# Log decays of a head: broadcast by a matmul, or copied over all partitions by DMA

## The reference, cut to what matters

```python
acs = jnp.cumsum(dtc * a.reshape(g, r), axis=2)          # log decay of every token
seg = acs_t[..., :, None] - acs_t[..., None, :]
decay_in = jnp.exp(jnp.where(lower, seg, -jnp.inf))       # 128 x 128 for one head
cb = jnp.einsum('bcign,bcjgn->bcgij', cc, bc)             # one for a group
y_diag = jnp.einsum('bcgij,bcgrij,bcjgrp->bcigrp', cb, decay_in, xdt)
```

## Time and profile before

| | |
|---|---|
| median of 3 runs | 2887.86 us (2879.88 to 2888.41) |
| the profiled execution | 2884.6 us, of which the span of the trace is 2882.7 us |
| TensorE, matmuls | 2811.8 us, 98% of the span |
| TensorE, weight loads | 2386.9 us, 83% |
| VectorE | 1769.8 us, 61% |
| ScalarE | 1483.7 us, 51% |
| GpSimd | 204.2 us, 7% |
| mean granted clock of TensorE | 0.995 |
| DMA | 594.25 MB, mean 206 GB/s |

### The profile page before, as it was taken

How to read it: one execution, slowest core, us unless ns; L and a number is a source line. 1 busy time by engine, 2 the same in 40 slices (tenths; PEclk the granted TensorE clock), 3 DMA queues, 4 the chain that set the end, 5 groups by cost and what they waited for, 6 DMA issues and landing times.

```text
span 2882.7 us, 41663 instructions
## 1 busy us (share of the span) xinstructions
PE 2811.8 (98%) x16960; PEld 2386.9 (83%) x16960; DVE 1769.8 (61%) x2255; ACT 1483.7 (51%) x2210; POOL 204.2 (7%) x259
## 2 busy tenths in 40 slices
PE   7999999999999999999899999999999999999998
PEld 4888998888777888877669889988887888897886
DVE  2487899886344445544355878998854444554555
ACT  3356776774333445533334567767743434544443
POOL 0001111120000000000100011111200000000000
PEclk9999999999999999999999999999999999999999
DMA  9945455546777644567796454555467565554665
GB/s 391 341 156 167 162 169 175 176 154 201 281 278 288 203 152 161 170 249 274 265 347 189 158 166 159 171 174 175 154 205 284 192 201 171 161 176 153 204 220 174
DMA packets 166591, 594.25 MB, mean 206 GB/s; under 512 B 20244, under 2 KB 22548, under 8 KB 166016
## 3 DMA queue, kind: packets, MB, share of 16 engines
q1 hardware_dynamic: 155376, 558.24, 56.3%
q0 software_dynamic: 10960, 33.34, 4.0%
q10 hardware_dynamic: 64, 0.02, 0.0%
HBM read 577.85 MB, written 13.66 MB: 205 GB/s over the span
## 4 chain that ended last, share of the span: by engine, by line
PE 84%; DVE 7%; DMA 5%; ACT 1%; issue 1%; SPq 0%; DVEq 0%; POOLq 0%; POOL 0%; ACTq 0%
PE PM L414 18%; PE PM L426 17%; PE PM L415 17%; PE PM L419 7%; PE PM L430 7%; PE PM L420 7%; PE A L639 5%; DVE w_l L392 2%; DVE arena L1368 2%; PE A L451 2%; DVE X L1408 2%; DMA Zt<-in_w_mod 2%; DMA raw<-in_w_in 2%; DMA raw<-in_w_out 1%; PE A L636 1%; PE PM L636 1%
## 5 line engine op out<-in xcount | busy, mean ns | idle before, releaser
L392 DVE TENSOR_TENSOR w_l<-raw,w_h 128x1024 fp32r<-128x1024 f32 (+1 forms) x880 | 1057.2, 1213 | 980.2 <-ACT w_h L387 971.4
L387 ACT ACTIVATE w_h<-raw 128x1024 fp32r<-128x1024 f32 (+1 forms) x880 | 903.6, 1046 | 837.9 <-PE PM L426 298.7
L414 PE MATMUL PM<-w_h,hT_h 128*128 128x512 f32 x1408 | 563.8, 400 | 2.2 <-issue 1.4
L415 PE MATMUL PM<-w_h,hT_l 128*128 128x512 f32 x1408 | 549.9, 391 | 0.0
L419 PE MATMUL PM<-hT_h,w_h 128*128 128x256 f32 x1920 | 486.4, 291 | 5.7 <-ACT w_h L387 2.5
L420 PE MATMUL PM<-hT_l,w_h 128*128 128x256 f32 x1920 | 469.7, 282 | 0.0
L414 PE MATMUL PM<-w_h,Z 128*128 128x512 f32 x1024 | 406.9, 397 | 12.7 <-ACT w_h L387 9.1
L415 PE MATMUL PM<-w_h,Z 128*128 128x512 f32 x1024 | 401.4, 392 | 0.0
L419 PEld LDWEIGHTS PM<-hT_h,w_h 128*128 128x128 f32 x1920 | 366.5, 191 | 20.6 <-issue 12.0
L426 PE MATMUL PM<-w_l,hT_h 128*128 128x512 f32 x1408 | 377.6, 390 | 0.7 <-DVE w_l L392 0.7
L420 PEld LDWEIGHTS PM<-hT_l,w_h 128*128 128x128 f32 x1920 | 367.2, 191 | 6.2 <-issue 4.8
(11 more groups left out here) (189 smaller groups left out, 2205.8 us busy)
## 6 DMA issues: line engine op xcount, KB each, us to landing
raw<-in_w_in SPq DMA_DIRECT2D x608, 512.0 KB, 4.0
raw<-in_w_ps SPq DMA_DIRECT2D x128, 512.0 KB, 5.0
raw<-in_w_mod SPq DMA_DIRECT2D x112, 512.0 KB, 4.1
Zt<-in_w_mod SPq DMA_DIRECT2D x80, 512.0 KB, 14.2
raw<-in_w_pa SPq DMA_DIRECT2D x64, 512.0 KB, 4.5
raw<-in_w_out SPq DMA_DIRECT2D x64, 512.0 KB, 6.0
arena<-in_states POOLq DMA_DIRECT2D x16, 512.0 KB, 3.8
out_state_f_out<-arena POOLq DMA_DIRECT2D x16, 256.0 KB, 2.8
```

The costliest lines, as they stand in the source:

```text
L387: act.activation(w_h[:, k % RING, :, 0:n], half_raw(k, n), ACT.Copy).then_inc(hi_ready, 1)
L392: dve.tensor_tensor(w_l[:, k % RING, :, 0:n], half_raw(k, n), w_h[:, k % RING, :, 0:n].bitcast(F32), ALU.subtract).then_inc(lo_ready, 1)
L414: pe.matmul(tok_out(s), hi[:, kt, tk], wh, start=kt == 0, stop=False, skip_group_check=True)
L415: pe.matmul(tok_out(s), lo[:, kt, tk], wh, start=False, stop=False, skip_group_check=True)
```

## The change

The broadcast of a head's log decays leaves TensorE. The rows are made once per layer without their second copy (4 matmuls fewer), ScalarE copies them from PSUM to `Hs` (64 partitions x 512) and stores them to a scratch tensor in HBM. For every head, GpSimd's queue then issues a DMA that reads the head's row of 2 KB and writes it to all 128 partitions of the buffer `E[h % 4]` (`decay_row`). `exp` reads and writes that buffer. Its step moves for heads 0 to 3 from 2 + h to 1 + h, so `exp(q, 0)` stands at 1, ahead of `z_silu`; heads 4 to 7 stay at 2 + h. The rows of heads 4 to 7 are issued when `y_diag` of head h - 4 is done, those of the next group's heads 0 to 3 at the end of `ssd_group`, ahead of the loading of its states. `squares` writes its unused output to `zs` in place of `E[0]`.

```diff
-                        for w in range(2):
-                            mm = fp32(A[NH * w:NH * w + NH, 0, ds * P:(ds + 1) * P], SA[:, 8 + ds, :], (Umat, Lmat)[ds // 2], ds == 0)
+                        mm = fp32(A[0:NH, 0, ds * P:(ds + 1) * P], SA[:, 8 + ds, :], (Umat, Lmat)[ds // 2], ds == 0)
...
-                def decay(q, h):
-
-                    if h == 0:
-                        pe.wait_ge(s_("H_ready"), L + 1)
-                        if q == 0:
-                            pe.wait_ge(s_("cb_even"), L * 4 + 4)
-                            pe.wait_ge(s_("cb_odd"), L * 4 + 4)
-                        else:
-                            pe.wait_ge(s_("st_stored"), L * NG + q)
-                    if h >= 2:
-                        pe.wait_ge(s_("exp_done"), (L * NG + q) * HG + h - 1)
-                    b = A[:, 2 + h % 2, :]
-                    mm = pe.matmul(b, sel[:, q * HG + h:q * HG + h + 1].to_broadcast([P, P]), H[:].rearrange("p d s n -> p (d s n)"),
-                                   start=True, stop=True, skip_group_check=True)
-                    mm.then_inc(s_("decay_done"), 1)
...
-                def H_hi():
+                def H_copy():
                     act.wait_ge(s_("acsT_done"), L + 1)
-                    act.activation(H[:].rearrange("p d s n -> p (d s n)"), A[:, 0, :], F.Copy).then_inc(s_("H_hi"), 1)
+                    act.activation(Hs[:], A[0:NH, 0, :], F.Copy).then_inc(s_("H_copied"), 1)
+                    act.wait_ge(s_("H_copied"), L + 1)
+                    act.dma_start(h_dram[L], Hs[:]).then_inc(s_("H_stored"), DMA)
...
                 def exp(q, h):
                     G = L * NG + q
-                    act.wait_ge(s_("decay_done"), G * HG + h + 1)
-                    if h >= 4:
-                        act.wait_ge(s_("y_part"), G * HG + h - 3)
+                    act.wait_ge(e_loaded[h % 4], (G * 2 + h // 4 + 1) * DMA)
                     e = E[h % 4]
                     for d in range(2):
                         for s in range(2):
-                            ins = act.activation(e[:, d, s, :], A[:, 2 + h % 2, (2 * d + s) * P:(2 * d + s + 1) * P],
-                                                 F.Relu, scale=-1.0, bias=SA[:, 2 * d + s, q * HG + h:q * HG + h + 1])
+                            ins = act.activation(e[:, d, s, :], e[:, d, s, :], F.Relu, scale=-1.0,
+                                                 bias=SA[:, 2 * d + s, q * HG + h:q * HG + h + 1])
...
                     for h in range(HG):
-                        st[2 + h] = [lambda h=h: exp(q, h)] + st.get(2 + h, [])
+                        at = 1 + h + h // 4
+                        st[at] = [lambda h=h: exp(q, h)] + st.get(at, [])
...
-                def H_lo():
-                    dve.wait_ge(s_("H_hi"), L + 1)
...
+                def decay_row(q, h):
+
+                    G = L * NG + q
+                    if q == 0 and h == 0:
+                        wait_alone(pool, s_("H_stored"), (L + 1) * DMA)
+                    if q or h >= 4:
+                        wait_alone(pool, s_("y_part"), G * HG + h - 3)
+                    row = h_dram[L, q * HG + h:q * HG + h + 1, :].to_broadcast([P, 4 * P])
+                    pool.dma_start(E[h % 4].rearrange("p d s n -> p (d s n)"), row).then_inc(e_loaded[h % 4], DMA)
+
                 def ssd_group(q):
...
                     ins.then_inc(s_("xw_ready"), 1)
+                    decay_row(q, 4)
                     if q:
                         wait_alone(pool, s_("yT_done"), G)
                     for s in range(2):
+                        if s:
+                            decay_row(q, 5)
...
                     ins.then_inc(s_("yD_ready"), 1)
+                    decay_row(q, 6)
+                    decay_row(q, 7)
                     if q < NG - 1:
+                        for h in range(4):
+                            decay_row(q + 1, h)
                         wait_alone(pool, s_("yoff_done"), G + 1)
                         load_states(q + 1)
```

More of the change, by code:

```diff
@@ L239, in build @@
         x_dram = nc.dram_tensor("x_scratch", (2, TOK, D_MODEL), F32).ap()
+        h_dram = nc.dram_tensor("log_decay_scratch", (DEPTH, NH, 4 * P), F32).ap()
         gate_dram = nc.dram_tensor("gate_scratch", (2, D_MODEL), F32).ap()
@@ L311, in build @@
         fng = part(2048, 5376)
-        sel32 = part(NH, 4864)
         modg = part(512, 0).rearrange("p (t n) -> p t n", t=2)
@@ L318, in build @@
         one = cst[0:P, K_U + P - 1:K_U + P]
-        sel = sb("sel", [P, NH], F32R)
         cond = sb("cond", [P, KT, 32])
@@ L326, in build @@
         SA = sb("SA", [P, NQ, NH])
-        H = sb("H", [P, 2, 2, P], F32R)
+        Hs = sb("Hs", [NH, 4 * P])
         half_exp = sb("half_exp", [P, 2])
@@ L338, in build @@
         raw_loaded = [sem(f"raw_loaded{i}") for i in range(SLOTS)]
+        e_loaded = [sem(f"e_loaded{i}") for i in range(4)]
         z_loaded = [sem(f"z_loaded{i}") for i in range(Z_SLOTS)]
@@ L744, in log_decays @@
                     pe.wait_ge(s_("chw_ready"), L + 1)
-                    pe.wait_ge(s_("const_cast"), 1)
                     fp32(A[:, 3, 0:256].rearrange("p (d s n) -> p d s n", d=2, s=2)[:, 0], Umat, SA[:, 8:10, :], True)
@@ L761, in cb @@
                         pe.wait_ge(s_("conv_silu"), L * 12 + 3)
-                        pe.wait_ge(s_("H_ready"), L + 1)
+                        pe.wait_ge(s_("H_copied"), L + 1)
                         pe.wait_ge(s_("tail_ready"), L + 1)
@@ L827, in final_states @@
                 def final_states(q):
-                    pe.wait_ge(s_("exp_done"), (L * NG + q) * HG + HG)
+                    if q:
+                        pe.wait_ge(s_("st_stored"), L * NG + q)
+                    else:
+                        pe.wait_ge(s_("cb_even"), L * 4 + 4)
+                        pe.wait_ge(s_("cb_odd"), L * 4 + 4)
                     pe.wait_ge(s_("xw_ready"), L * NG + q + 1)
@@ L845, in ssd_steps @@
                     for h in range(HG):
-                        st[h] = [lambda h=h: decay(q, h)] + st.get(h, [])
                         st[4 + h] = st.get(4 + h, []) + [lambda h=h: y_diag(q, h)]
@@ L1089, in layer @@
                       33: [lambda: bc_silu(0), lambda: center(1)], 36: [lambda: bc_silu(1), lambda: center(2)],
-                      38: [H_hi], 39: [lambda: bc_silu(2)]}
+                      38: [H_copy], 39: [lambda: bc_silu(2)]}
                 if L == 0:
@@ L1098, in layer @@
                     xT_copy(3)
-                    act.wait_ge(s_("masks_loaded"), DMA)
-                    act.activation(sel[:], sel32, F.Copy).then_inc(s_("const_cast"), 1)
                     h_hi(0)
@@ L1168, in squares @@
                             ch.wait()
-                        ch.link(act.activation(E[0].rearrange("p d s n -> p (d s n)"), y[:, s], F.Square, accum_out=ss[:, s:s + 1]))
+                        ch.link(act.activation(zs[:, s], y[:, s], F.Square, accum_out=ss[:, s:s + 1]))
                     ch.wait()
@@ L1518, in cumulative @@
                         .then_inc(s_("tail_ready"), 1)
-                def H_lo():
-                    dve.wait_ge(s_("H_hi"), L + 1)
-                    Hl = H[64:128].rearrange("p d s n -> p (d s n)")
-                    tt(Hl, A[64:128, 0, :], Hl.bitcast(F32), ALU.subtract).then_inc(s_("H_ready"), 1)
                 def decay_dt():
@@ L1530, in layer @@
                       34: [lambda: conv_bc(1, 0)], 35: [lambda: conv_bc(1, 1)], 37: [lambda: conv_bc(2, 0)],
-                      38: [lambda: conv_bc(2, 1)], 39: [H_lo, cumulative]}
+                      38: [lambda: conv_bc(2, 1)], 39: [cumulative]}
                 if L == 0:
@@ L1857, in _ @@
                 pool.dma_start(x2[:, s], v).then_inc(s_("x_loaded"), DMA)
-            pool.dma_start(sel32, a["cst"][:, K_SEL:K_WIDTH]).then_inc(s_("masks_loaded"), DMA)
             wait_alone(pool, s_("half_exp_set"), 1)
@@ L1930, in layer @@
                 load_states(0)
+                for h in range(4):
+                    decay_row(0, h)
                 for g in range(NG):
```

## The result

The changed kernel took 2971.49 us (median of 4 runs, 2970.32 to 2973.63), the kernel before 2888.14 us. The ratio is 1.0297, with a 95% interval of 1.0284 to 1.0309: 83 us slower. The forecast was 30 us slower, 2918 us, with 2944 us as the upper end. The direction and the places of the waits came out as written; their size did not.

What follows compares the result with a forecast made beforehand. A loop through saturated VectorE and ScalarE and TensorE's equally long queue both limit. Twelve longer bodies (+28.8 us), group 7 (+3.4), less 1 give +31: 2915.6 us profiled, stated as 2918, range 2868 to 2944.

Steps and rivals of the forecast that it cites:

- A body is 2.4 us longer: SSD stage, groups 1 to 6: table loads and row waits together lengthen each body by 2.4 us at x = 4.0.
- the 1.7 us for group 7: Group 7 runs into a TensorE-bound stage and keeps some 1.7 us of its stall, +3.4 us for two.
- A body is what passes from S to VectorE's half 4, plus 41.7 us: From S, a body's start, to half 4's subtraction, then 41.7 us of saturated VectorE and ScalarE, sets a body's length.
- 1.7 us later: Two more table loads a body on ScalarE delay VectorE's half 4 from S + 14.15 to S + 15.8.
- x = 4.0: Extra wait for a row's DMA before exponentials of heads 4 to 7: 4.0 us, including 3.5 us of landing.
- TensorE ends half 7 at S + 30.9 and `y_diag(q, 3)` at S + 31.25: TensorE's times after cast 7 at S + 27.7 and VectorE's half 7 at S + 29.9; S is the body's start.
- The sum: Twelve bodies +28.8 us, group 0 nothing, group 7 +3.4, less 1: +31 us; +21 at x = 3.3, +55 at 5.0.
- All of 29.4 us comes back: Rival: TensorE, not VectorE's waits, is the bound, so removing 128 matmuls saves all their time: 2858 us; 6%.
- stay hidden: Rival: table loads stay hidden and rows land by 3.3 us, so half 4 comes earlier: -15 us, 2872 us; 17%.
- even: Rival: gain and loss meet because VectorE's queue is less rigid than read, 2880 to 2896 us; 13%.
- Slow rows: Rival: rows take 7.3 us to land, halves 7 and 10 both late, 9.7 us a body, 3010 us; 6%.
- Bodies are 58 us apart: Sign expected in the profile: SSD bodies 58 us apart instead of 55.9.

Runs made afterwards that it cites:

- narrow: The kernel before with its broadcast matmuls 32 columns wide instead of 512, apart from heads 0 and 1 of group 0; 2880.8 us.
- order_eight: The changed kernel with eight buffers E instead of four and every head's exponential at half 2 + h, the old order; 2872.8 us.
- eight: The changed kernel with eight buffers E instead of four, so that every row is loaded a whole body ahead; 2905.6 us.
- ahead2: The changed kernel with eight buffers, the next group's exponentials 0 and 1 at halves 11 and 12, heads 2 to 7 at half h, M from half 1; 2871.3 us.
- fill: The changed kernel with eight matmuls that nobody reads in TensorE's gap ahead of half 7; 2961.7 us.
- z_first: The changed kernel, four buffers, with z_silu ahead of exp(q, 0), so two table loads a body instead of four; 2949.1 us.
- eight_z: The changed kernel with eight buffers E instead of four and z_silu ahead of exp(q, 0); 2879.4 us.
- later: The changed kernel, four buffers, with the exponentials of heads 4 to 7 one half later, behind the casts of halves 7 to 10; 2916.7 us.

## Why the prediction was wrong in size

The mechanism was the one that was written: more table loads ahead of VectorE's half 4, and two waits for a row with a cast behind each. The step that failed is "**A body is 2.4 us longer**". It is 5.9 us longer, and half 10 comes at S + 41.9 instead of S + 38.3. These 3.6 us are VectorE's stretch ahead of half 4 (1.1), half 7 at TensorE's lower clock, a term that the prediction doesn't have (1.3), head 7's row (0.6), and steps of 0.1 to 0.2 us between them (0.6). In the sum this and the 1.7 us for group 7 make some 50 of the 56 us by which the profiled execution was missed. The steps in turn:

**"A body is what passes from S to VectorE's half 4, plus 41.7 us"; the 29.4 us aren't worth more than the other loop lets through:** right. `narrow` took off 15 us of TensorE and gave 6, `order_eight` took off all of them and gave 15. In both, VectorE's half 4 starts sooner, at S + 13.8 and S + 13.5 instead of S + 14.15, where fewer broadcasts stand ahead of `xt_T`. A body is 55.6 and 55.3 us instead of 55.9, and the fourteen intervals between the stores are 4 and 8 us shorter in sum. The first bodies of the two layers give 1 and 3 us more. The rest of the 15 us, some 5, lies outside the SSD stages, where the traces differ by more than this among themselves: from the last store of the first layer to the first body of the second pass 1002.7 us in `eight` (676.16 to 1678.83) and 1011.1 us in `ahead2` (657.51 to 1668.62), whose edits leave this stretch alone.

**"1.7 us later" for the table loads:** the mechanism was right, the size too small. Cast 3 began 0.4 us later than worked out: the four Relus of two heads now read SBUF and take 1.28 us instead of 1.16, and an Exp with a load behind it takes 0.65 us instead of 0.54. The 4.94 us on VectorE became 5.6: the addition at the end of `y_off` took 1.43 us instead of 0.7 while GpSimd's `xw` (426.44 to 428.49 us) ran beside it; before, `xw` ran beside half 4. So S + 16.9 instead of S + 15.8. The move was to cost 12 x 1.7 = 20 us and cost 33, of which the loads are 22 to 26.

**"x = 4.0" for the DMA in the path:** near at the first wait, too small at the second. `exp(q, 4)` began 4.48 us after `y_diag(q, 0)` gave way, against 0.29 + 4.0 worked out. GpSimd's DMA started 0.80 us after it, as worked out (0.29 + 0.5), and the row landed in 3.7 us, where I took 3.5. `exp(q, 7)` began 4.86 us after `y_diag(q, 3)`, with a row that took 4.05 us. The median of all copies is 4.1.

**"TensorE ends half 7 at S + 30.9 and `y_diag(q, 3)` at S + 31.25":** this is where most of it went wrong. Cast 7 was there at S + 29.3 instead of S + 27.7, most of it the 1.1 us above, and then half 7 ran at the lower clock. `y_diag(q, 3)` gave way at S + 34.2. A row that took 4.1 us instead of 3.5 followed, and half 10 came at S + 41.9 instead of S + 38.3. I had costed TensorE's idle time by its length alone. The gap was on the path of the next wait, and a slower half 7 was inside the cycle from one row to the next. `fill` puts some 10 us on the clock, and bodies of the changed kernel without the fall agree, at about 1 us each. Even in such a body half 10 came at S + 40.5, so the clock is less than half of the error.

**The sum:** twelve bodies at 2.4 us and two end groups at 1.7 should have been fourteen at 5.8. Group 7's steps run beside the next stage, but its half 10 is as late as any other's: the interval that holds it is 61.3 us (648.17 to 709.49) against 55.9. I had let it keep 1.7. This step is worth 8 us. Group 0, put at nothing, made the first body of a layer 1.5 and 1.9 us longer (56.6 and 56.9 us against 55.05). And by its own terms the sum's ends are +23 at x = 3.3 and +53 at x = 5.0, not +21 and +55; this changes nothing of the outcome.

**The price of an error at x.** Between the start of the body and half 10 there are two waits, and each takes in what was late before it. By the working of the prediction the second costs nothing below about 3.3 us, and above it every tenth goes through. The forecast stood near this bend, and all its errors (0.4 + 0.7 + 1.3 + 0.6, and the small ones) had the same sign.

**The rivals.** "All of 29.4 us comes back", "stay hidden" and "even" are out. "Slow rows" was the nearest in time and wrong in mechanism: 88 of the 128 rows landed in 3.3 to 4.4 us, 10.1 at most. "Stay hidden" had its two conditions met in `order_eight`, which has two loads a body and rows in time: its sum, 2872 us, is within 1 us of what that kernel took, in part by luck, since some 5 us of the gain lie outside these stages. What was to be seen in the profile was seen: four loads a body, waits of 5.2 to 7.8 us ahead of `exp(q, 4)` and 2.3 to 4.4 us ahead of `exp(q, 7)` where "about 4" was written for both, gaps ahead of half 7. "Bodies are 58 us apart" was 61.7.

**The Trainium skill beside the runs.** The Trainium skill's "ScalarE: Activation LUTs", section "Rules for kernel authors", asks to do all functions of one table set before switching: with this rule `z_first` and `eight_z` agree, where two loads fewer in a body save 22 and 26 us. It budgets about 2.7 us for a switch. The rows show 1.28 us for a load and under 0.05 us around it. The Trainium skill's "DMA: Bandwidth & Descriptors", section "Anatomy of one DMA — SWDGE (gpsimd) path", has a fit of 2.0 us plus the bytes at 436 GB/s, an estimate of 2.6 us for these 256 KB. The measured median is 4.1 us, beside weight loads that bring the DMA to some 190 GB/s.

What stays open: when the clock falls. At half 7 it fell in 10 of 16 groups of the changed kernel and in 9 of `z_first`, and the length of the gap ahead of it doesn't decide: in `z_first` it stayed at 1.00 behind a gap of 3.07 us (at 377.2 us).

## What to carry to other kernels

A busy share of 98% does not say that an engine sets the time: follow the chain of waits through one period, and look for a stretch in which another engine has no gap. When a step gets a DMA into its inputs, look at what stands behind the step in its engine's queue; in this kernel that was most of the cost: an order that puts the next cast first (`later`), or a buffer more so that the copy is issued early (`eight`), took most of it away. And when exponentials are moved past a function of another table set, count the loads.

The best versions here are `ahead2` and `order_eight`, 0.5% faster than the kernel before.

## What was not expected of the hardware

TensorE's granted clock fell behind a gap of 2.04 us between long stretches of matmuls: the next half ran at 0.21 us a matmul instead of 0.12, until about 445 us. Gaps of 0.56 and 0.98 us in the same body left it at 1.00. So did gaps of 2.13 and 2.21 us in other bodies of the same kernel (at 2050.1 and 626.9 us), so a gap's length alone doesn't tell. Eight matmuls in the long gap kept the clock up at half 7 in 15 of 16 groups, where it fell in 10 of 16 without them, so that a kernel with more work was not slower.
